# Six weight units of a decoder layer split in halves, one evacuation that signals apart, one update ahead of a subtraction

## The chip, the cores and the metric

The kernel runs on one core of one Trainium2 chip. The metric is the device time of one launch in microseconds (us); three launches of the kernel before gave a median of 1365.99 us (1365.53 to 1366.52).

## What is computed

One decoder layer in float32 on 256 tokens of width 2048. Three token mixers read one input projection; their outputs are gated, merged, projected and normalised, and a mixture of 16 experts follows:

```python
h = x @ w_in[l]
(q_a, k_c, v_c, k_s, v_s, k_w, v_w, g_nsa, q_b, c_kv, q_idx, k_idx, w_idx,
 uv, g_merge) = _split_cols(h, IN_SPLITS)
...
y = jnp.einsum('bsnw,nwd->bsnd', branches, w_branch[l])
gates = jax.nn.sigmoid(g_merge.astype(jnp.float32)).astype(x.dtype).reshape(B, S, N_BRANCHES, D)
mixed = jnp.sum(gates * y, axis=2) @ w_out[l]
x = _layer_norm(DEEPNORM_ALPHA * x + mixed, ln1_g[l], ln1_b[l])
ffn = _hier_moe(x, router_group_w[l], router_group_b[l], router_expert_w[l], router_expert_b[l],
                expert_w_gate[l], expert_w_up[l], expert_w_down[l])
x = _layer_norm(DEEPNORM_ALPHA * x + ffn, ln2_g[l], ln2_b[l])
```

Inside the first mixer, blocks of 32 keys and of 32 values are each compressed by a product of 4096 values with `cmp_w1` (`jax.nn.gelu(xb @ w1) @ w2`).

## The kernel before

**Units.** Up to the experts, every weight is read in units of 128 x 2048 float32 (1 MB). A unit passes four stations. SyncE (SP) loads it into one of six slots of `raw`. ScalarE (ACT) copies it to `whi` as fp32r, the high part (`hi`, L1470). VectorE (DVE) subtracts, `wlo = raw - whi`, the low part (`lo`, L1699). TensorE (PE) multiplies: each product is three matmuls, high by high, high by low and low by high (`mm3`, L1065 to L1067). `whi` and `wlo` have two slots each, so the copy of unit u waits until PE has used unit u - 2.

**Signals.** `landed` counts loads, `hi_done` copies, `lo_done` subtractions, `unit_used` units that PE has finished. PE waits for `lo_done` before a unit (`unit_ready`). Unit 0 alone is already worked in quarters, with the semaphores `part_hi` and `part_lo` (`first_part`, L1574 and L1824), and PE waits for a quarter in the middle of that unit.

**Order.** Each engine runs a program written out by hand. First come 13 chunks of the input projection (NCH = 13), of four units each but for one: ckv (units 0 to 3), small (4), kcvc (5 to 8), slc (9 to 12), then four units of `cmp_w1` (13 to 16, `w1u` = 13), win (17 to 20), and qa0 to u1. A unit of a chunk is 48 matmuls of 256 columns or 24 of 512, a unit of `cmp_w1` only 12 of 512 columns. Chunks alternate between two accumulators, `main[0]` and `main[1]`. When PE has finished a chunk, ACT moves it out (`evacuate`) and increments `chunk_out`. The last chunk, u1, is moved out by two gelus (L1509) from `main[0]`; then the loop of steps begins.

**Steps.** For each of three branches b and four blocks i of 512 columns, `step(b, i)` multiplies four units of gate columns into `main[1]` and two units of `w_branch` into `main[0]`. At its start PE waits for `chunk_out` >= NCH + 4b + i. After its first unit PE computes attention scores (L1272), which need `qst`, two copies that ACT makes at the head of its own step (L1629). In the fifth position DVE adds sigmoid times product to the merged sum `acc` (L1932, L1933), after the low part of the unit two ahead, and increments `step_free`. Branches 0 and 1 run in hardware loops, and so do three steps of the last branch; its last step is written out (there `i` is a Python integer).

**Output projection and experts.** Unit U1 is the first of `w_out`. After it PE transposes the last columns of the merged sum (`merged(3)`, L1338), which waits for `step_free`. The experts (`moe_pe`) stream 192 units of 1 MB through a ring of places; SP loads a unit when PE has used the one that lay there (`m_used`).

Two lines that decide the first waits of a step, on PE and on DVE:

```python
pe.wait_ge(chunk_out, NCH + it + i)
dve.wait_ge(chunk_out, NCH + 1 + 4 * b + i)
```

Of the kernel before, what the change touches and what calls it, by code (L numbers as in the profile page):

```python
# [17 lines left out]
F32, F32R, I32 = mybir.dt.float32, mybir.dt.float32r, mybir.dt.int32  # L18
# [40 lines left out]
UNIT = 2048  # L59
# [28 lines left out]
def build(nc, A, out):  # L88
# [14 lines left out]
    with ExitStack() as ctx:  # L103
        def sem(name):
            return ctx.enter_context(nc.semaphore(name))
# [38 lines left out]
        UB = QUADS + 2  # L144
        BR = [2, 0, 1]
        U1 = U0 + NB * 4 * UB
        assert UB % RAW == 0 and UB % SPLIT == 0

        def last(name):
# [144 lines left out]

        landed = [sem(f"landed{j}") for j in range(RAW)]
        hi_done, lo_done, unit_used = sems("hi_done lo_done unit_used")
        chunk_out = sem("chunk_out")
        step_free = sem("step_free")

        pch, ach, dch = sems("pch ach dch")  # L300
# [742 lines left out]
        def _(pe):  # L1043
# [34 lines left out]
            def unit_ready(u):  # L1078
                pe.wait_ge(lo_done, u + 1)

            def start_chunk(name):
                c = chunks[name][0]
                if c >= 2:
                    pe.wait_ge(chunk_out, c - 1)
                return main[c % 2], chunks[name][1]
# [17 lines left out]
            def mixed_chunk(name, f0, t0, hook=None):  # L1103

                ps, u0 = start_chunk(name)
                for q in range(QUADS):
                    u = u0 + q
                    if u:
                        unit_ready(u)
                    if u and name == "ckv":  # L1110
                        pe.wait_ge(x_lo, 2 * q + 2)
                    wh, wl = view(whi, u % SPLIT, 4, 512), view(wlo, u % SPLIT, 4, 512)
                    for kk in range(4):
                        k = 4 * q + kk
                        if u == 0:
                            if kk % 2 == 0:
                                pe.wait_ge(x_lo, kk // 2 + 1)
                            if kk < 3:
                                pe.wait_ge(part_lo, kk + 1)
                            else:  # L1120
                                unit_ready(0)
                        for m in range(2):
                            c = f0 + m * P
                            features(ps[:, 0, m * S:(m + 1) * S], k, wh[:, kk, c:c + P], wl[:, kk, c:c + P],
                                     k == 0 and m == 0, k == KT - 1, True)
                        for t in range(T):
                            ins = tokens(ps[:, 1, t * 256:(t + 1) * 256], k, t, wh[:, kk, t0:t0 + 256],
                                         wl[:, kk, t0:t0 + 256], k == 0 and t == 0, k == KT - 1, True)
                        if u == 0 and kk == 1:
                            x_transposes(range(2, 4))  # L1130
                    ins.then_inc(unit_used, 1)
                    if hook:
                        hook(u)
# [67 lines left out]
            for j, (xh, xl) in enumerate(((xpkh, xpkl), (xpvh, xpvl))):  # L1201
                pe.wait_ge(xp_lo, j + 1)
                for q in range(2):
                    u = w1u + 2 * j + q
                    unit_ready(u)
                    wh, wl = view(whi, u % SPLIT, 16, P), view(wlo, u % SPLIT, 16, P)
                    for l in range(0, 16, LB):
                        cols = slice((q * 16 + l) * KV * NC, (q * 16 + l + LB) * KV * NC)
                        ins = mm3(att[0:LB * KV * NC, 3 - 2 * j, :], xh[:, cols], xl[:, cols],
                                  wh[:, l:l + LB, :].rearrange("p l m -> p (l m)"),  # L1210
                                  wl[:, l:l + LB, :].rearrange("p l m -> p (l m)"), q == 0 and l == 0,
                                  q == 1 and l == 16 - LB)
                    ins.then_inc(unit_used, 1)
# [128 lines left out]
            def step(b, i):  # L1342
                ub, it = U0 + b * 4 * UB, 4 * b
                src = (o1, o2, o1)[b]
                g, y = NCH % 2, (NCH + 1) % 2
                for j in range(UB):
                    u = ub + j
                    if j == 0:
                        pe.wait_ge(chunk_out, NCH + it + i)
                    if j == QUADS:  # L1350
                        pe.wait_ge(step_free, 1 + it + i)
                        if b == 2:
                            pe.wait_ge(att_free, 9)
                    pe.wait_ge(lo_done, u + 1 + i * UB)
                    wh, wl = view(whi, u % SPLIT, 4, 512), view(wlo, u % SPLIT, 4, 512)
                    for kk in range(4):
                        for t in range(T):
                            if j < QUADS:
                                k = 4 * j + kk
                                ins = tokens(main[g][:, t, :], k, t, wh[:, kk, :], wl[:, kk, :], k == 0, k == KT - 1)  # L1360
                            else:
                                k = 4 * (j - QUADS) + kk
                                cols = slice(t * P, (t + 1) * P)
                                ins = mm3(main[y][:, t, :], src[:, 0, k, cols], src[:, 1, k, cols],
                                          wh[:, kk, :], wl[:, kk, :], k == 0, k == HEADS - 1)
                    ins.then_inc(unit_used, 1)
                    if b == 0:
                        if j == 0:
                            pe.wait_ge(att_free, 1 + i)
                            scores(1 + i, True)  # L1370
                        if j == 3:
                            transposes(1 + i, True)
                        if j == 4:
                            values(1 + i, True)
                    if b == 1:
                        if j == 0:
                            pe.wait_ge(att_free, 5 + i)
                            latent_kv(i, 1 + i)
                        if j == 1:
                            pe.wait_ge(kh_out, 1 + i)  # L1380
                            pe.wait_ge(vh_out, 1 + i)
                            scores(5 + i, False)
                        if j == 3:
                            transposes(5 + i, False)
                        if j == 4:
                            values(5 + i, False)
                    if b == 2 and isinstance(i, int) and j < 3:
                        merged(j)
# [26 lines left out]
                    ins.then_inc(lt_ps, 1)  # L1415


            pe.wait_ge(chunk_out, NCH + 12)
            for c in range(4):
                ps = main[(NCH + c) % 2]  # L1420
                if c >= 2:
# [40 lines left out]
        def _(act):  # L1462
# [9 lines left out]
            def hi_at(u):  # L1472
                if u == SMALL:
                    act.wait_ge(gn_in, 16)
                hi(u, u % RAW, n=(KT * NSM if u == SMALL else UNIT), wait=u - SPLIT + 1 if u >= SPLIT else None)

            def evacuate(name):
# [28 lines left out]
                else:  # L1506
                    for j in range(2):
                        g = int(name[1]) * 4 + j * 2
                        ins = act.activation(flat(uT[:, g:g + 2, :]), ps[:, j, :], ACT.Gelu_apprx_tanh)  # L1509
                    ins.then_inc(chunk_out, 1)  # L1510

            after = {}
            for name in chunks:
# [180 lines left out]
        def _(dve):  # L1694
# [5 lines left out]
                                  ALU.subtract).then_inc(lo_done, 1)  # L1700

            def lo_at(u):
                lo(u, u % RAW, u + 1, KT * NSM if u == SMALL else UNIT)

            def qseg(tensor, q):
# [132 lines left out]
                    x_part(2 * u + 3)  # L1838
                extra(u)
            lo_at(U0)  # L1840
            dve.wait_ge(chunk_out, NCH)
            dve.tensor_tensor(mixt[:, 4:8, :], mixt[:, 4:8, :], uT[:, 4:8, :], ALU.mult).then_inc(mix_u, 1)
            lo_at(U0 + 1)
            dve.wait_ge(oc_hi, 1)
# [54 lines left out]
                                      mhi[dst].rearrange("p k s -> p (k s)").bitcast(F32), ALU.subtract).then_inc(m_lo, 1)  # L1899

            def step(b, i):
                for j in range(UB):
                    u = U0 + b * 4 * UB + j + 2
                    lo(u, u % RAW, u + 1 + i * UB)
                    if b == 0:
                        if j == 0:
# [10 lines left out]
                    if b < 2 and j == 4:  # L1917
# [3 lines left out]
                            ins = dve.tensor_tensor(dst[:, 1, bass.ds(4 * a + i, 1), :].rearrange("p a s -> p (a s)"), att[:, a, 0:S],  # L1921
                                                    dst[:, 0, bass.ds(4 * a + i, 1), :].rearrange("p a s -> p (a s)").bitcast(F32), ALU.subtract)
                        ins.then_inc(att_free, 1)
                    if j == 5:
                        dve.wait_ge(chunk_out, NCH + 1 + 4 * b + i)
                        dve.wait_ge(unit_used, u - 1 + i * UB)
                        a_ = acc[:, :, bass.ds(i * 512, 512)]
                        y = main[(NCH + 1) % 2]
                        if b == 0:
                            dve.tensor_tensor(a_, sig[:], y[:], ALU.mult).then_inc(step_free, 1)  # L1930
                        else:
                            link(dve.tensor_tensor(sig[:], sig[:], y[:], ALU.mult))  # L1932
                            dve.tensor_tensor(a_, a_, sig[:], ALU.add).then_inc(step_free, 1)  # L1933
                    if b == 2 and isinstance(i, int) and 1 <= j < 4:
                        merged(j - 1)

# [30 lines left out]
```

## Time and profile before

| | us |
|---|---|
| median of 3 runs | 1365.99 |
| the profiled execution, its own time | 1364.78 |
| its span | 1362.8 |
| PE busy | 1321.0 (97%) |
| weight loads of PE busy, 7311 of them (beside the matmuls) | 967.0 (71%) |
| DVE busy | 581.8 (43%) |
| ACT busy | 482.2 (35%) |
| granted PE clock, mean | 0.995 |

The span is the time between the first and the last instruction that the profiler saw; the launch's own time is 2.0 us more. Busy time counts instructions that run; a wait is idle time, and the profile names the instruction that ended it. A row of the timeline gives start, duration, engine, line and tiles, and in brackets the idle time before it with its releaser. Ends of matmuls are modelled, so the spacing of their starts says more than their durations.

### The profile page before, as it was taken

What the parts mean: (1) busy time and instruction counts of PE and PEld (TensorE: products, weight loads), DVE (VectorE), ACT (ScalarE), POOL (GpSimd) and SP (SyncE); (2) the same over time, 40 slices, a digit from 0 to 9 for tenths busy, and PEclk for the clock granted to TensorE, in tenths of its full rate; (3) what the DMA queues carried; (4) which work ended last, traced back from release to release, by engine and by line L of the source; (5) the groups of instructions that cost most, each with busy time, mean ns of one, the idle gap of its engine ahead of it and who ended that gap; (6) DMA issues with size and microseconds to landing.
All of it is one profiled execution on the core that took longest, in us unless ns stands there. A gap on an engine that the chain in (4) does not pass through costs nothing.

```text
span 1362.8 us, 17747 instructions
## 1 busy us (share of the span) xinstructions
PE 1321.0 (97%) x7311; PEld 967.0 (71%) x7311; DVE 581.8 (43%) x738; ACT 482.2 (35%) x658; POOL 27.5 (2%) x45
## 2 busy tenths in 40 slices
PE   8999999999999999999999999999999999999895
PEld 8989989998888888888888878854443443544341
DVE  4377445445546535545454554525121120211206
ACT  4544334335455544545333433331111111211111
POOL 0000000400000000000100001000000000000000
PEclk9999999999999999999999999999999999999998
DMA  9767555544444356545556795699999999999995
GB/s 302 257 191 240 185 185 186 186 156 157 156 150 154 124 169 189 166 168 169 183 187 194 274 381 202 241 372 388 412 421 421 422 421 421 422 419 422 421 404 194
DMA packets 120460, 364.94 MB, mean 268 GB/s; under 512 B 11528, under 2 KB 17096, under 8 KB 96336
## 3 DMA queue, kind: packets, MB, share of 16 engines
q1 hardware_dynamic: 114080, 359.58, 71.1%
q10 hardware_dynamic: 6320, 4.49, 1.1%
q8 instruction: 46, 0.75, 0.2%
q14 instruction: 14, 0.11, 0.0%
HBM read 361.95 MB, written 2.10 MB: 267 GB/s over the span
## 4 chain that ended last, share of the span: by engine, by line
PE 90%; DMA 5%; DVE 2%; ACT 1%; issue 1%; DVEq 0%; SPq 0%; ACTq 0%
PE main L1065 19%; PE main L1067 18%; PE main L1066 18%; PE main L501 14%; PE att L567 6%; DMA mraw<-in_expert_w_down_dram 5%; PE att L458 4%; PE att L1304 1%; PE att L1272 1%; PE main L470 1%; PE main L471 1%; PE att L550 1%; PE att L1287 1%; ACT whi L1470 1%; PE att L1323 1%
## 5 line engine op out<-in xcount | busy, mean ns | idle before, releaser
L1699 DVE TENSOR_TENSOR wlo<-raw,whi 128x2048 fp32r<-128x2048 f32 (+1 forms) x140 | 321.9, 2299 | 371.4 <-ACT whi L1470 371.4
L1470 ACT ACTIVATE whi<-raw 128x2048 fp32r<-128x2048 f32 (+1 forms) x140 | 267.6, 1911 | 430.9 <-PE main L1067 423.9
L501 PE MATMUL main<-mraw,xg 128*64 128x512 f32 x1024 | 225.0, 594 | 0.1
L1065 PE MATMUL main<-whi,xhi 128*128 128x512 f32 (+1 forms) x544 | 203.5, 374 | 1.3 <-ACT uT L1509 1.3
L1067 PE MATMUL main<-whi,xlo 128*128 128x512 f32 (+1 forms) x544 | 201.7, 371 | 0.0
L1066 PE MATMUL main<-wlo,xhi 128*128 128x512 f32 (+1 forms) x544 | 201.5, 370 | 0.0
L501 PEld LDWEIGHTS main<-mraw,xg 128*64 128x64 f32 x1024 | 71.9, 137 | 135.9 <-issue 134.6
L1065 PE MATMUL main<-xhi,whi 128*128 128x256 f32 (+1 forms) x560 | 159.6, 285 | 2.2 <-DVE wlo L1699 1.1
L1066 PE MATMUL main<-xlo,whi 128*128 128x256 f32 (+1 forms) x560 | 158.4, 283 | 0.0
L1067 PE MATMUL main<-xhi,wlo 128*128 128x256 f32 (+1 forms) x560 | 158.4, 283 | 0.0
L1065 PEld LDWEIGHTS main<-whi,xhi 128*128 128x128 f32 x544 | 102.6, 189 | 18.4 <-issue 1.5
L1067 PEld LDWEIGHTS main<-whi,xlo 128*128 128x128 f32 x544 | 102.5, 188 | 17.8
L1066 PEld LDWEIGHTS main<-wlo,xhi 128*128 128x128 f32 x544 | 102.6, 189 | 17.0
L1065 PEld LDWEIGHTS main<-xhi,whi 128*128 128x128 f32 (+1 forms) x560 | 106.9, 191 | 4.0 <-DVE wlo L1699 1.5
L1066 PEld LDWEIGHTS main<-xlo,whi 128*128 128x128 f32 (+1 forms) x560 | 106.9, 191 | 0.0
L1067 PEld LDWEIGHTS main<-xhi,wlo 128*128 128x128 f32 (+1 forms) x560 | 106.9, 191 | 0.0
L567 PE MATMUL att<-mraw,hT 128*64 128x512 f32 x448 | 98.6, 594 | 3.9 <-DMA mraw<-in_expert_w_down_dram 3.4
L608 ACT ACTIVATE xg<-att,gbT 128x128 f32<-128x128 f32 x128 | 47.3, 465 | 133.0 <-PE att L458 132.7
L567 PEld LDWEIGHTS att<-mraw,hT 128*64 128x64 f32 x448 | 31.9, 137 | 66.2 <-issue 62.8
L755 DVE TENSOR_TENSOR out_acc<-out_acc,main 128x512 f32<-128x512 f32 x64 | 41.4, 684 | 83.4 <-PE main L471 67.1
L1065 PE MATMUL main<-whi,o 128*128 128x512 f32 x192 | 76.4, 398 | 0.0
L1067 PE MATMUL main<-whi,o 128*128 128x512 f32 x192 | 74.9, 390 | 0.0
(319 smaller groups left out, 1352.7 us busy)
## 6 DMA issues: line engine op xcount, KB each, us to landing
raw<-in_w_in_dram SPq DMA_DIRECT2D x95, 1024.0 KB, 5.0
mraw<-in_expert_w_gate_dram SPq DMA_DIRECT2D x64, 1024.0 KB, 19.2
mraw<-in_expert_w_up_dram SPq DMA_DIRECT2D x64, 1024.0 KB, 20.8
mraw<-in_expert_w_down_dram SPq DMA_DIRECT2D x64, 1024.0 KB, 17.7
raw<-in_w_branch_dram SPq DMA_DIRECT2D x24, 1024.0 KB, 5.1
raw<-in_w_out_dram SPq DMA_DIRECT2D x16, 1024.0 KB, 7.0
xin<-in_x_dram SPq DMA_DIRECT2D x4, 512.0 KB, 8.1
out_dram<-out_acc SPq DMA_DIRECT2D x8, 256.0 KB, 2.0
```

The costliest lines, as they stand in the source:

```text
L458: ins = pe.matmul(att[:, q, k % 4 * P:(k % 4 + 1) * P], xr[:, t, k * P:(k + 1) * P], hot[:, t, :], start=(k % 4 == 0 and t == 0), stop=(t ...
L470: pe.matmul(main[1][:, n % 2, :], rows, yhi[:, c % 2, :], start=True, stop=False)
L471: pe.matmul(main[1][:, n % 2, :], rows, ylo[:, c % 2, :], start=False, stop=True).then_inc(sc_ps, 1)
L501: ins = pe.matmul(main[0][half, w, :], xg[:, k, half], src[:, kk * DE:(kk + 1) * DE], start=(k == 0), stop=(k == KT - 1))
L567: ins = pe.matmul(att[half, c, :], hT[:, f, half], src[:, c * 512:(c + 1) * 512], start=(f == 0), stop=(f == DE // P - 1))
L608: ins = act.activation(xg[:, k, :], att[:, q, k % 4 * P:(k % 4 + 1) * P], ACT.Identity, bias=gbT[:, KT + k:KT + k + 1], scale=gbT[:, k:k + 1])
L755: dve.tensor_tensor(out_acc[:, t, cols], out_acc[:, t, cols], main[1][:, n % 2, :], ALU.add).then_inc(sc_free, 1)
L1065: pe.matmul(o, ah, bh, start=start, stop=False, skip_group_check=skip)
L1066: pe.matmul(o, ah, bl, start=False, stop=False, skip_group_check=skip)
L1067: return pe.matmul(o, al, bh, start=False, stop=stop, skip_group_check=skip)
L1470: act.activation(whi[:, u % SPLIT, 0:n], raw[:, slot, 0:n], ACT.Copy).then_inc(hi_done, 1)
L1699: dve.tensor_tensor(wlo[:, u % SPLIT, 0:n], raw[:, slot, 0:n], whi[:, u % SPLIT, 0:n].bitcast(F32), ALU.subtract).then_inc(lo_done, 1)
```

## The change

Three edits. Unit 1, the four units of `cmp_w1` and the first unit of win (`HALVED`, units 1 and 13 to 17) are copied, subtracted and waited for in two halves of 1024 columns; the first halves signal through `part_hi` and `part_lo`, whose counts go on from unit 0's. The evacuation of u1 increments a semaphore of its own, `u1_out`, and every later count of `chunk_out` is one less. In the step that is written out, DVE's update of the merged sum stands before the subtraction of the unit it followed.

```diff
+        HALVED = [1, *range(w1u, w1u + 5)]
...
+            def half_ready(u, half):
+
+                if half == 0 and u in HALVED:
+                    pe.wait_ge(part_lo, 4 + HALVED.index(u))
+                else:
+                    unit_ready(u)
...
-                        unit_ready(u)
+                        half_ready(u, 0)
...
+                        if kk == 2 and u in HALVED:
+                            half_ready(u, 1)
...
-                    unit_ready(u)
                     wh, wl = view(whi, u % SPLIT, 16, P), view(wlo, u % SPLIT, 16, P)
                     for l in range(0, 16, LB):
+                        if l % 8 == 0:
+                            half_ready(u, l // 8)
...
-                        pe.wait_ge(chunk_out, NCH + it + i)
+                        pe.wait_ge(chunk_out, NCH - 1 + it + i)
...
+                if u in HALVED:
+                    act.wait_ge(landed[u % RAW], 16 * (u // RAW + 1))
+                    if u >= SPLIT:
+                        act.wait_ge(unit_used, u - SPLIT + 1)
+                    for cols, done in ((slice(0, UNIT // 2), part_hi), (slice(UNIT // 2, UNIT), hi_done)):
+                        act.activation(whi[:, u % SPLIT, cols], raw[:, u % RAW, cols], ACT.Copy).then_inc(done, 1)
+                    return
...
-                    ins.then_inc(chunk_out, 1)
+                    ins.then_inc(u1_out if name == "u1" else chunk_out, 1)
...
-            dve.wait_ge(chunk_out, NCH)
+            dve.wait_ge(u1_out, 1)
...
                 for j in range(UB):
                     u = U0 + b * 4 * UB + j + 2
+                    if j == 5 and isinstance(i, int):
+                        update(u)
                     lo(u, u % RAW, u + 1 + i * UB)
...
+                    if j == 5 and not isinstance(i, int):
+                        update(u)
```

`lo_at` has a loop like that of `hi_at`, with two subtractions. `update` holds DVE's two products as they stood.

**ACT, behind unit 14.** The queue from the end of slc's evacuation (`vs`) to the copy of unit 18; `cT` is a transposed latent. Before:

```order
L1494 ACTIVATE vs<-main 128x512
L1470 ACTIVATE whi<-raw 128x2048 [waits unit_used,landed3]
L1538 ACTIVATE cT<-att 128x512 [waits c_ps]
L1470 ACTIVATE whi<-raw 128x2048 [waits unit_used,landed4]
L1470 ACTIVATE whi<-raw 128x2048 [waits unit_used,landed5]
L1470 ACTIVATE whi<-raw 128x2048 [waits unit_used,landed0]
```

Now:

```order
L1512 ACTIVATE vs<-main 128x512
L1491 ACTIVATE whi<-raw 128x1024 [waits unit_used,landed3]
L1491 ACTIVATE whi<-raw 128x1024
L1556 ACTIVATE cT<-att 128x512 [waits c_ps]
L1491 ACTIVATE whi<-raw 128x1024 [waits unit_used,landed4]
L1491 ACTIVATE whi<-raw 128x1024
L1491 ACTIVATE whi<-raw 128x1024 [waits unit_used,landed5]
L1491 ACTIVATE whi<-raw 128x1024
L1481 ACTIVATE whi<-raw 128x2048 [waits unit_used,landed0]
```

Each copy of the units 15, 16 and 17 has become two, with the waits on the first of the two; what stands between the units stands where it did.

**DVE, in the last step.** The queue around the update of the merged sum (`sig`, then `acc`); `mlo` is the low part of the merged sum, transposed. Before:

```order
L1699 TENSOR_TENSOR wlo<-raw,whi 128x2048 [waits hi_done] x2
L1932 TENSOR_TENSOR sig<-sig,main 128x1024 [waits unit_used,chunk_out]
L1933 TENSOR_TENSOR acc<-acc,sig 128x2x512 [waits dch]
L1699 TENSOR_TENSOR wlo<-raw,whi 128x2048 [waits hi_done]
L1898 TENSOR_TENSOR mlo<-att,mhi 128x512 [waits m_hi] x2
```

Now:

```order
L1717 TENSOR_TENSOR wlo<-raw,whi 128x2048 [waits hi_done]
L1936 TENSOR_TENSOR sig<-sig,main 128x1024 [waits unit_used,chunk_out]
L1937 TENSOR_TENSOR acc<-acc,sig 128x2x512 [waits dch]
L1717 TENSOR_TENSOR wlo<-raw,whi 128x2048 [waits hi_done] x2
L1923 TENSOR_TENSOR mlo<-att,mhi 128x512 [waits m_hi] x2
```

The subtraction of unit U1 + 1 has gone from ahead of the two products to behind them.

## Rows read from the trace of the kernel before

**Rows 1.** Waits of PE over the whole span: us in total, times, longest.

```profile
PE att L1065 <- DVE wlo L1699: 2.9, 2, 1.5
...
PE att L1338 <- DVE acc L1933: 1.3, 1, 1.3
PE main L1065 <- ACT uT L1509: 1.3, 1, 1.3
PE main L1065 <- DVE wlo L1699: 1.1, 1, 1.1
```

**Rows 2.** Windows: length; busy us of PE, PEld, DVE, ACT, POOL; clock, DMA share, GB/s.

```profile
895.00:900.00 5.00, 5.00 (x25) 1.44 (x21) 0.00 (x0) 0.00 (x0) 0.00 (x0) 1.00 0.43 144
...
950.00:960.00 10.00, 10.00 (x54) 4.82 (x52) 1.28 (x2) 1.50 (x4) 0.00 (x0) 1.00 0.87 341
...
1180.00:1190.00 10.00, 10.00 (x59) 5.07 (x58) 0.48 (x1) 1.50 (x4) 0.00 (x0) 1.00 1.01 422
```

**Rows 3.** Timeline around unit 1, PE, ACT and DVE, 8 to 24 us.

```profile
12.98 1.91 ACT L1470 ACTIVATE whi<-raw 128x2048 fp32r<-128x2048 f32 x1
...
14.93 2.29 DVE L1699 TENSOR_TENSOR wlo<-raw,whi 128x2048 fp32r<-128x2048 f32 x1 [1.00 <-ACT whi L1470]
...
17.27 0.39 PE L1065 MATMUL main<-xhi,whi 128*128 128x256 f32 x1 [1.11 <-DVE wlo L1699]
...
20.03 2.29 DVE L1699 TENSOR_TENSOR wlo<-raw,whi 128x2048 fp32r<-128x2048 f32 x1 [1.61 <-ACT whi L1470]
...
23.92 0.36 PE L1065 MATMUL main<-xhi,whi 128*128 128x256 f32 x1
```

**Rows 4.** Timeline over the units 14 to 17, PE, ACT and DVE, 91 to 106 us.

```profile
91.13 1.92 ACT L1470 ACTIVATE whi<-raw 128x2048 fp32r<-128x2048 f32 x1 [4.30 <-PE main L1067]
...
93.08 2.29 DVE L1699 TENSOR_TENSOR wlo<-raw,whi 128x2048 fp32r<-128x2048 f32 x1 [1.79 <-ACT whi L1470]
...
95.43 0.50 PE L1065 MATMUL att<-whi,xpkh 128*120 128x512 f32 x1 [1.50 <-DVE wlo L1699]
...
102.87 0.49 PE L1065 MATMUL att<-whi,xpvh 128*120 128x512 f32 x1 [1.39 <-DVE wlo L1699]
...
105.96 0.35 PE L1065 MATMUL main<-xhi,whi 128*128 128x256 f32 x1
```

**Rows 5.** Timeline: operations of 960 columns on ACT and DVE, at 81 to 91 us.

```profile
80.86 0.99 ACT L1535 ACTIVATE xpkh<-xpk 128x960 fp32r<-128x960 f32 x1
...
90.14 1.15 DVE L1773 TENSOR_TENSOR xpvl<-xpv,xpvh 128x960 fp32r<-128x960 f32 x1
```

**Rows 6.** Timeline of PE inside unit 0: the second row begins its second quarter.

```profile
9.81 0.28 PE L1067 MATMUL main<-whi,xlo 128*128 128x256 f32 x1
9.93 0.28 PE L1065 MATMUL main<-xhi,whi 128*128 128x256 f32 x1
```

**Rows 7.** Timeline where the steps begin, PE and ACT, 318 to 326 us.

```profile
318.29 1.09 ACT L1509 ACTIVATE uT<-main 128x512 f32<-128x512 f32 x2 [3.78 <-PE main L1067]
...
319.51 0.49 PE L1065 MATMUL main<-whi,xhi 128*128 128x512 f32 x1 [1.26 <-ACT uT L1509]
...
324.30 0.73 ACT L1629 ACTIVATE qst<-qaT 128x256 f32 x2
...
325.17 0.89 PE L1272 MATMUL att<-ksT,qst 128*128 128x128 f32 x4
```

**Rows 8.** Timeline around the last step's end, ACT, DVE and PE, 784 to 792 us.

```profile
784.31 1.92 ACT L1470 ACTIVATE whi<-raw 128x2048 fp32r<-128x2048 f32 x1 [3.52 <-PE main L1067]
...
786.26 2.29 DVE L1699 TENSOR_TENSOR wlo<-raw,whi 128x2048 fp32r<-128x2048 f32 x1 [3.15 <-ACT whi L1470]
788.47 1.21 DVE L1932 TENSOR_TENSOR sig<-sig,main 128x1024 f32<-128x1024 f32 x1
789.72 1.23 DVE L1933 TENSOR_TENSOR acc<-acc,sig 128x1024 f32<-128x1024 f32 x1
...
791.00 1.09 PE L1338 MATMUL att<-ident,acc 128*128 128x128 f32 x8 [1.34 <-DVE acc L1933]
```

More of the change, by code:

```diff
@@ L296, in build @@
         hi_done, lo_done, unit_used = sems("hi_done lo_done unit_used")
-        chunk_out = sem("chunk_out")
+        chunk_out, u1_out = sem("chunk_out"), sem("u1_out")
         step_free = sem("step_free")
@@ L1415, in route @@
                     ins.then_inc(lt_ps, 1)
-            pe.wait_ge(chunk_out, NCH + 12)
+            pe.wait_ge(chunk_out, NCH + 11)
             for c in range(4):
@@ L1702, in lo_at @@
             def lo_at(u):
+                if u in HALVED:
+                    for cols, made_, value, done in ((slice(0, UNIT // 2), part_hi, 4 + HALVED.index(u), part_lo),
+                                                     (slice(UNIT // 2, UNIT), hi_done, u + 1, lo_done)):
+                        dve.wait_ge(made_, value)
+                        dve.tensor_tensor(wlo[:, u % SPLIT, cols], raw[:, u % RAW, cols], whi[:, u % SPLIT, cols].bitcast(F32),
+                                          ALU.subtract).then_inc(done, 1)
+                    return
                 lo(u, u % RAW, u + 1, KT * NSM if u == SMALL else UNIT)
@@ L1901, in step, with update @@
             def step(b, i):
+                def update(u):
+                    dve.wait_ge(chunk_out, NCH + 4 * b + i)
+                    dve.wait_ge(unit_used, u - 1 + i * UB)
+                    a_ = acc[:, :, bass.ds(i * 512, 512)]
+                    y = main[(NCH + 1) % 2]
+                    if b == 0:
+                        dve.tensor_tensor(a_, sig[:], y[:], ALU.mult).then_inc(step_free, 1)
+                    else:
+                        link(dve.tensor_tensor(sig[:], sig[:], y[:], ALU.mult))
+                        dve.tensor_tensor(a_, a_, sig[:], ALU.add).then_inc(step_free, 1)
                 for j in range(UB):
                     u = U0 + b * 4 * UB + j + 2
+                    if j == 5 and isinstance(i, int):
+                        update(u)
                     lo(u, u % RAW, u + 1 + i * UB)
@@ L1923, in step @@
                         ins.then_inc(att_free, 1)
[L1924 to L1933, printed above, removed]
+                    if j == 5 and not isinstance(i, int):
+                        update(u)
                     if b == 2 and isinstance(i, int) and 1 <= j < 4:
```

## The prediction

> **What bounds the kernel now.** I read the waits of PE first. PE is busy 97% of the span, so only its idle time can go, and up to the experts its list holds few waits: 2.9 us in two waits of `cmp_w1` units for their low part, 1.1 in one wait of a unit of ckv for the same, 1.3 where the steps begin, for a gelu of u1, and 1.3 where the transposes of the merged sum wait for DVE's last product [rows 1]. That is 6.6 us in all, and the change touches every one of them. The first question is which of them really go.
>
> The second question is whether time won early arrives at the end, and for that I read the windows of the expert stage. There the DMA engines are the pace: at 1180 us they move 422 GB/s at a share of 1.01, while between 895 and 900 us they moved 144 GB/s and between 950 and 960 us 341 [rows 2]. So the stream has holes at its start, where SP waits for places that PE has yet to free, and runs without them later. A stream that starts to run full when PE lets it start moves with PE. All of its gates (units used of `w_out`, places used by the first experts) lie behind the four waits. I therefore carry every microsecond won before 800 us through to the end, one for one.
>
> **Unit 1.** The whole copy starts at 12.98 and takes 1.91, the subtraction starts at 14.93 and takes 2.29, and PE starts at 17.27 after 1.11 idle, so it was ready at 16.16 [rows 3]. For a half of 1024 columns I take the rows of 960 columns, 0.99 on ACT and 1.15 on DVE [rows 5], and between these and the rows of 2048 columns about 1.04 and 1.22. The first half is then low at 12.98 + 1.04 + 1.22 + 0.05 for the handoff = 15.3, before 16.16. The second half follows some 1.2 behind it, at 16.5, and PE wants it half a unit after its start, at 19: unit 2 starts 6.65 after unit 1, with eight transposes between, so a unit of 48 matmuls takes about 5.8. The wait goes whole: 1.1. What is late next is unit 2, whose subtraction ends at 20.03 + 2.29 = 22.32 because its copy came late; PE started it at 23.92 and will want it at 22.8 [rows 3]. There is 0.5 us left, so nothing is given back.
>
> **Units 13 to 17.** The copy of unit 14 starts at 91.13, when PE has released the slot, the subtraction at 93.08, and PE starts at 95.43, 1.50 late, so it was ready at 93.93 [rows 4]. With halves the first is low at 91.13 + 1.04 + 1.22 + 0.05 = 93.4 and the second at about 94.6. PE reaches the second half six matmuls later, at half of the 3.09 that a unit takes from its start to the next unit's (102.87 to 105.96, [rows 4]), thus at 95.5. Both are in time, by 0.5 and 0.9. From here on a slot is released a unit earlier relative to the old chain. The copy of unit u starts when unit u - 2 ends, its first half is low 2.3 later, and PE wants it 3.09 later: a margin of 0.7 per unit, where the whole chain of 1.92 + 2.29 = 4.2 missed by 1.1. That covers units 15 and 16, and also unit 17, which before had the time that the wait of unit 16 gave it and would now be the next late one if it were whole. Unit 18 is whole, but PE works unit 17, a long one, for 5.8, more than 4.2. So both waits go: 1.50 + 1.39 = 2.9. I take off 0.1 for the break that PE keeps at a unit's start and book 2.8.
>
> The splits add one instruction per unit on ACT and on DVE, twelve in all. Between 960 and 2048 columns ACT's time grows by 0.93 us and DVE's by 1.14 for 1088 columns [rows 3, 5], so a column costs 0.85 and 1.05 ns and the part that does not grow is 0.17 and 0.14 us. That is at most 0.3 us per unit, and it lies beside PE: with 2.1 us of ACT and 2.4 of DVE in the 3.09 of a unit both queues have room.
>
> PE gets six more waits in the middle of a unit. Unit 0 has such waits already: its second quarter begins 0.12 after the matmul before, the spacing inside a quarter [rows 6]. I book nothing; the upper bound is one weight load uncovered at each, 0.13 us by the page (967.0 us in 7311 loads), 0.8 in all. The Trainium skill, "TensorE: Matmul & The Clock Gate", section on queue depths, says that PE's queue can pull weight loads ahead of matmuls in flight. If a wait closed that window, each of the six would cost up to such a load, and the sum would be 4.4; rows 6 speak against it.
>
> **The signal of u1.** Step 0 writes `main[1]`, whose chunk u0 was moved out long before, so PE no longer waits for the gelus and starts at 318.25 in place of 319.51. That looks like 1.26 us. But the step's first unit is followed by the scores, and these need `qst`. ACT's way there is one chain that starts at u1's end and that the edit leaves alone: two gelus from 318.29, a copy, the high part of the mixed output, a table load, and the two `qst` copies, 324.30 + 0.73 = 325.03. PE's scores ran at 325.17 [rows 7]. Before, PE and ACT met there by chance. Now PE is there 1.26 earlier, at 323.9, and waits 1.2 us for ACT. What is late next is `qst`, and I book 0 us, within bounds of 0 and 1.3. I take the lower end because ACT's chain has no gap that PE's start could close.
>
> **The merged sum.** PE's unit U1 - 1 ends at 784.3, where ACT's copy of unit U1 + 1 is released [rows 8]. DVE idles then. Before, it waited for that copy, subtracted from 786.26, and only then ran the products, 788.47 and 789.72 to 790.95; PE had waited 1.34 when it started at 791.00, so it was ready at 789.66. Now the products run at 784.35 to 786.85 and the subtraction from 786.9 to 789.15. PE finds the sum 2.8 us before it wants it, and its next unit's low part 1.6 us before it wants that (789.66 + 1.09 = 790.75). The gain is 1.3. The subtraction ends 0.6 later, and SP's next load of `w_out`, which waits for it, starts 0.6 later, for a unit that is due five units on.
>
> **Sum.** 1.1 + 2.8 + 0 + 1.3 = 5.2 us. The profiled execution, 1364.78, would be 1359.6. It is 1.2 below the median, and a difference carries over: 1365.99 - 5.2 = **1360.8**.
>
> **The rivals.** *The first signal pays in full.* If `qst` were not the gate, because PE's own time to the scores is longer than I read or ACT starts earlier, the 1.3 of rows 7 would come on top: 1359.5. The 0.14 us between `qst` and the scores is all that speaks for it.
>
> *The halves move their waits.* My margins in units 14 to 17 are 0.5 to 0.9 us per unit. The Trainium skill, "VectorE: DVE Perf Modes", section on the trn2 errata, says that many small tiles each pay a fixed latency that one large tile pays once; rows 5 agree with some 0.15 us. If copies and subtractions do not overlap as I laid them out and each half arrives 0.7 late, the waits shrink to about a half and unit 17 gets one: 1.4 of 2.8 is lost, and 1362.2 comes out.
>
> *The expert stream does not follow.* If its start is set by something that does not move with PE (its own queue at 800 us, say), the end stays where it is, 1366. The holes of rows 2 speak against it.
>
> *Slower.* The stream's holes grow. The one between 950 and 960 us costs 10 x (1 - 341/422) = 1.9 us [rows 2]. PE now meets the ring of places at another phase of SP's waits, and a place freed late in each expert pair would open one more such hole per pair. Against a gain of 5.2 it takes (5.2 + 2.7) / 1.9, thus more than four new holes, to come out slower; with five, 1365.99 - 5.2 + 9.5 = 1370.3. Nothing in the trace shows a hole once PE is well ahead.
>
> **How the numbers follow.** About 0.2% (2.7 us, thus 1363.3) is what a measurement can tell from no change. Forecast 0.68; first signal in full 0.09; waits moved 0.11; stream does not follow 0.09; slower 0.03. The first three are faster: 0.88; the fourth is the same, 0.09. The range holds the first three with the bounds of the mid-unit waits and half a microsecond of scatter: 1359.0 to 1363.0.
>
> **What would show it.** PE's list of waits should have lost the waits for `wlo` at units 1, 14 and 16 and the one for `acc`. The wait for uT should be gone too, and a new one of about 1.2 us stand before the scores, for `qst` on ACT: this is the sharpest sign. The unit that follows the `cmp_w1` units should start 3.9 us earlier than before, at 102.1. The stream should again show 422 GB/s at 1180 us and end 5 us earlier. A wait on `part_lo` in units 14 to 17, or breaks of 0.2 us in their middle, would show the halves mis-sized. No new wait before the scores, with a span 6.5 us shorter, would show my reading of `qst` wrong; an unchanged end of the stream would break the step that carries gains through.

## The result, and the profile after

The changed kernel took 1358.36 us (median of 4, 1357.47 to 1358.89) against 1366.13 for the kernel before (median of 4); the ratio is 0.9947 with a 95% interval of 0.9935 to 0.996, so 5.5 to 8.9 us faster. The forecast of 1360.8 named the places of the gain rightly, but the time lies 0.6 us below the low end of its range. The profiled execution took 1358.89, the longest of the four, with a span of 1357.2 against 1362.8.

The list of PE's waits, over the whole span, answers to [rows 1]. Of the four groups there, none is left; one wait is new:

```profile
PE main L538 <- DVE hh L764: 8.6, 8, 1.1
...
PE att L1283 <- ACT qst L1647: 1.5, 1, 1.5
PE main L1066 <- DVE wlo L1849: 1.0, 1, 1.0
```

The wait for `wlo` L1849 is unit 0's and stood in the trace before too. The new one, for `qst`, is where the forecast put it, and it takes the whole gain of the first signal.

Timeline of the changed kernel around unit 1, against [rows 3] (start, duration, engine, line, tiles):

```profile
13.21 2.01 ACT L1491 ACTIVATE whi<-raw 128x1024 fp32r<-128x1024 f32 x2
...
14.31 2.36 DVE L1725 TENSOR_TENSOR wlo<-raw,whi 128x1024 fp32r<-128x1024 f32 x2
...
15.35 1.04 PE L1056 MATMUL att<-ident,xin 128*128 128x128 f32 x8
16.14 0.36 PE L1066 MATMUL main<-xhi,whi 128*128 128x256 f32 x1
...
18.13 1.92 ACT L1481 ACTIVATE whi<-raw 128x2048 fp32r<-128x2048 f32 x1 [1.06 <-DMA raw<-in_w_in_dram]
```

Two halves of a copy take 2.01 in place of 1.91, two of a subtraction 2.36 in place of 2.29: the split costs 0.1 and 0.07 us, less than the bound of 0.3 for both. PE goes from the transposes into unit 1 without idle time.

The same over the `cmp_w1` units, the first matmul of each of the units 13 to 17, against [rows 4]:

```profile
89.74 0.47 PE L1066 MATMUL att<-whi,xpkh 128*120 128x512 f32 x1
...
92.61 0.39 PE L1066 MATMUL att<-whi,xpkh 128*120 128x512 f32 x1
...
95.41 0.46 PE L1066 MATMUL att<-whi,xpvh 128*120 128x512 f32 x1
...
98.28 0.39 PE L1066 MATMUL att<-whi,xpvh 128*120 128x512 f32 x1
...
101.06 0.30 PE L1066 MATMUL main<-xhi,whi 128*128 128x256 f32 x1
```

A unit now takes 2.8 to 2.9 us from start to start, about twelve times 0.233, the usual spacing of these matmuls. The five starts span 11.32 us; before, from 90.90 to 105.96 [rows 4], they spanned 15.06. That is 3.74 us, where the sum booked 2.8. Unit 17, which the forecast expected at 102.1 us, starts at 101.06. Two places of the kernel before, in its own timeline, show what the list of waits had left out:

```profile
93.55 0.39 PE L1067 MATMUL att<-whi,xpkl 128*120 128x512 f32 x1
95.43 0.50 PE L1065 MATMUL att<-whi,xpkh 128*120 128x512 f32 x1 [1.50 <-DVE wlo L1699]
95.77 0.39 PE L1066 MATMUL att<-wlo,xpkh 128*120 128x512 f32 x1
...
96.04 2.29 DVE L1699 TENSOR_TENSOR wlo<-raw,whi 128x2048 fp32r<-128x2048 f32 x1 [0.67 <-ACT whi L1470]
...
98.08 0.40 PE L1067 MATMUL att<-whi,xpkl 128*120 128x512 f32 x1
98.48 0.46 PE L1065 MATMUL att<-whi,xpvh 128*120 128x512 f32 x1
```

The idle time of 1.50 is counted from the modelled end of a matmul, 93.55 + 0.39. But the next start was due 0.23 after the last, at 93.78, so 1.65 us were lost. The matmul behind it starts 0.34 us later, where 0.23 is usual. At 98.48 no wait is listed, and the start is 0.17 late all the same: PE was due at 98.31, and DVE had unit 15's low part ready at 96.04 + 2.29 = 98.33.

Where the steps begin, against [rows 7]:

```profile
313.34 1.09 ACT L1527 ACTIVATE uT<-main 128x512 f32<-128x512 f32 x2 [3.78 <-PE main L1068]
...
316.12 1.92 ACT L1619 ACTIVATE o<-mixt 128x2048 fp32r<-128x2048 f32 x1
318.06 1.28 ACT L1647 ACT_TABLE_LOAD   x1
319.35 0.73 ACT L1647 ACTIVATE qst<-qaT 128x256 f32 x2
...
320.22 0.89 PE L1283 MATMUL att<-ksT,qst 128*128 128x128 f32 x4 [1.45 <-ACT qst L1647]
```

ACT's chain from u1's end to `qst` is as long as before (6.74 us from 313.34 to 320.08; before, 318.29 to 325.03), and PE starts the scores 0.14 behind it, as before.

At the last step's end, against [rows 8]:

```profile
779.51 1.22 DVE L1936 TENSOR_TENSOR sig<-sig,main 128x1024 f32<-128x1024 f32 x1 [1.21 <-PE main L1068]
780.77 1.23 DVE L1937 TENSOR_TENSOR acc<-acc,sig 128x1024 f32<-128x1024 f32 x1
781.91 2.28 DVE L1717 TENSOR_TENSOR wlo<-raw,whi 128x2048 fp32r<-128x2048 f32 x1
...
784.69 1.04 PE L1349 MATMUL att<-ident,acc 128*128 128x128 f32 x8
```

The transposes no longer wait. The expert stream again runs at 423 GB/s at 1180 us, against 422 in [rows 2]:

```profile
1180.00:1190.00 10.00, 10.00 (x58) 4.88 (x56) 2.05 (x9) 1.84 (x6) 0.00 (x0) 1.00 1.02 423
```

### The profile page after: what moved, and what is told of

The parts are those of the page before. It is cut to its first block, busy times and chain, and to the rows that moved or that the text cites. A ratio compares the mean times of both kernels' runs of the same rounds, so it can differ in the third digit from the quotient of the medians.

```text
span 1357.2 us, 17759 instructions
## 1 busy us (share of the span) xinstructions
PE 1321.8 (97%) x7311; PEld 969.0 (71%) x7311; DVE 582.3 (43%) x744; ACT 483.3 (36%) x664; POOL 27.5 (2%) x45
## 4 chain that ended last, share of the span: by engine, by line
PE 92%; DMA 5%; DVE 1%; ACT 1%; issue 1%; DVEq 0%; SPq 0%; ACTq 0%
PE main L1066 19%; PE main L1068 19%; PE main L1067 19%; PE main L502 14%; PE att L568 6%; DMA mraw<-in_expert_w_down_dram 5%; PE att L459 4%; PE att L1315 1%; PE att L1283 1%; PE main L471 1%; PE main L472 1%; PE att L551 1%; PE att L1298 1%; PE att L1334 1%; PE att L1330 1%
## 5 line engine op out<-in xcount | busy, mean ns | idle before, releaser
L1717 DVE TENSOR_TENSOR wlo<-raw,whi 128x2048 fp32r<-128x2048 f32 x134 | 308.1, 2299 | 359.5 <-ACT whi L1481 359.5
L1481 ACT ACTIVATE whi<-raw 128x2048 fp32r<-128x2048 f32 x134 | 256.3, 1913 | 418.1 <-PE main L1068 416.3
L756 DVE TENSOR_TENSOR out_acc<-out_acc,main 128x512 f32<-128x512 f32 x64 | 41.4, 684 | 83.7 <-PE main L472 67.2
```

The source lines that it names most:

```text
L756: dve.tensor_tensor(out_acc[:, t, cols], out_acc[:, t, cols], main[1][:, n % 2, :], ALU.add).then_inc(sc_free, 1)
L1481: act.activation(whi[:, u % SPLIT, 0:n], raw[:, slot, 0:n], ACT.Copy).then_inc(hi_done, 1)
L1717: dve.tensor_tensor(wlo[:, u % SPLIT, 0:n], raw[:, slot, 0:n], whi[:, u % SPLIT, 0:n].bitcast(F32), ALU.subtract).then_inc(lo_done, 1)
```

## The experiments

Each kernel was timed against the kernel before on the same chip. The first theory (the forecast's) takes listed waits, 1.1, 2.8, 0 and 1.3; the second, formed on the trace after, takes starts. From the start of unit 0 the traces give, in us, the start of: unit 13, unit 17, the scores, the transposes of the merged sum, and the router's first matmul (the fold, L425 or L426):

| trace | unit 13 | unit 17 | scores | transposes | fold |
|---|---|---|---|---|---|
| before | 82.47 | 97.53 | 316.74 | 782.57 | 871.30 |
| changed | 81.08 | 92.40 | 311.56 | 776.03 | 864.71 |
| halves only | 81.12 | 92.40 | 311.55 | 777.39 | 866.14 |
| signal only | 82.48 | 97.57 | 316.80 | 782.62 | 871.37 |
| update only | 82.48 | 97.53 | 316.74 | 781.07 | 869.75 |

So up to the fold the three edits give 5.16, -0.07 and 1.55 us, 6.64 together, and the changed kernel 6.59 (6.7 and 6.8 when it was traced again). Up to there traces of one kernel agree within 0.2: the kernel before, traced again, gave 82.47, 97.56, 316.78, 782.73 and 871.47.

**The changed kernel again, twice** (no edit).

> The changed kernel as it stands, timed again beside the others. If its profile tells the whole gain, its median lies some 5.6 us (the difference of the two profiled spans) below the kernel before; if the executions that were not profiled hold some 2 us more than the waits show, it lies 7 to 8 us below.

> The changed kernel a third time, beside the next one on the same chip. By the start-to-start theory (1.2 + 3.7 + 0 + 1.4) it stands 6.3 us below the kernel before; its first two measurements gave 7.2 and 7.9. If the rest is scatter of the expert stage, this one may fall on either side of 6.3 to 8; if it is a gain of its own, it stays above 7.

Measured: 1357.89 us against 1365.81, ratio 0.9942 (0.9929 to 0.9956), then 1357.76 against 1365.32, ratio 0.9942 (0.9928 to 0.9956). With the first measurement the ratios give 7.2, 7.9 and 7.9 us. The listed-wait sum of 5.2 is outside all three intervals (the nearest bound is 5.5). The 6.6 of the starts is inside all three, but each value lies above it.

**Only the halves.**

```diff
-                    ins.then_inc(u1_out if name == "u1" else chunk_out, 1)
+                    ins.then_inc(chunk_out, 1)
...
-                    if j == 5 and isinstance(i, int):
-                        update(u)
...
-                    if j == 5 and not isinstance(i, int):
+                    if j == 5:
                         update(u)
```

(and each count of `chunk_out` one higher again).

> Only the six units in halves; the signal of u1 and the order of the last step as before. The start-to-start readings of the changed trace give 1.2 us at unit 1 and 3.7 us at the units 13 to 16, so 4.9 us faster. My prediction's terms give 3.9. If the halves hold the part that was missed, 6 or more.

Measured: 1359.43 us, ratio 0.9959 (0.9946 to 0.9973), thus 5.6 us (3.7 to 7.4). The interval alone does not part 4.9 from 3.9 or from 6; the trace does, with 5.16 at the fold. That is over three quarters of the 6.6 of the whole change.

**Only the signal.**

```diff
-        HALVED = [1, *range(w1u, w1u + 5)]
+        HALVED = []
```

and the order of the last step as before.

> Only the signal of u1 apart. By the theory that qst takes the place of the gelu as the gate: 0 us, with a new wait of 1.2 to 1.5 us before the scores. By the rival that the signal pays: 1.3 us faster and no such wait.

Measured: 1364.99 us, ratio 0.9997 (0.9988 to 1.0006), 0.4 us within -0.8 and 1.6. The interval still holds the rival's 1.3, so the trace has to decide. It has the swap with nothing else moving: the wait for the gelu is gone from PE's list, and this stands there:

```profile
PE att L1283 <- ACT qst L1647: 1.4, 1, 1.4
```

The scores start 316.80 us after unit 0, where they started at 316.74 before. The signal by itself brings nothing.

**Only the update, twice.** `HALVED = []` and the counts of `chunk_out` as before.

> Only the update of the merged sum ahead of the subtraction in the last step. By the theory: 1.3 us faster. If the expert stream takes some of it, or the last step holds the missed 2 us, less than 1 or more than 2.5.

> Only the update moved, again: by the theory 1.4 us faster; if the 2.2 us of its first measurement are a gain of its own in the expert stage, 2 or more again.

Measured: 1363.3 us, ratio 0.9984 (0.9975 to 0.9993), then 1363.28, ratio 0.9986 (0.9977 to 0.9995), thus 2.2 and 1.9 us. The traces show 1.55 and 1.56 at the fold. Both times agree with that; neither excludes 0.5 us more.

**The units 13 to 17, and 13 to 16.**

```diff
-        HALVED = [1, *range(w1u, w1u + 5)]
+        HALVED = [*range(w1u, w1u + 5)]
```

and for the second kernel `w1u + 4`, both with the signal and the update as before.

> Only the units 13 to 17 in halves, nothing else. Start-to-start theory: 3.7 us faster. My prediction's term: 2.8.

> Only the units 13 to 16 in halves, unit 17 whole. By the theory that unit 17 becomes the next late one: its copy starts when unit 15 ends, some 100 us, and it is low 4.3 later, while PE wants it after 2.8, so a new wait of about 1.4 us stands before win, and 2.3 us are gained of the 3.7. By the rival that unit 17 did not need it: 3.7.

Measured: 1361.57 us, ratio 0.9971 (0.9959 to 0.9983), 4.0 us (2.3 to 5.6); and 1363.63, ratio 0.9988 (0.9979 to 0.9997), 1.6 us (0.4 to 2.9). The first interval does not part 3.7 from 2.8; the second excludes 3.7. In the first trace unit 17 starts 93.82 after unit 0, in the second 95.62, and in the kernel before 97.53: gains of 3.71 and 1.91. Unit 17 is in the list for a reason. In the second trace it is the next late unit (DVE's subtractions of the units 17 and 18, PE's last matmul of unit 16 and its start of unit 17):

```profile
101.48 2.29 DVE L1717 TENSOR_TENSOR wlo<-raw,whi 128x2048 fp32r<-128x2048 f32 x1 [1.34 <-ACT whi L1481]
104.27 2.29 DVE L1717 TENSOR_TENSOR wlo<-raw,whi 128x2048 fp32r<-128x2048 f32 x1 [0.49 <-ACT whi L1481]
...
101.83 0.40 PE L1068 MATMUL att<-whi,xpvl 128*120 128x512 f32 x1
103.92 0.36 PE L1066 MATMUL main<-xhi,whi 128*128 128x256 f32 x1 [1.69 <-DVE wlo L1717]
```

The wait that was moved is listed with 1.69, where I had put 1.4, and start to start it is 1.86 (103.92 less 101.83 and 0.23). I had let unit 17's copy start together with unit 16; it began at 99.54, 0.27 us after unit 16's first matmul. Unit 18, whole in both, starts on time.

**A delay ahead of the steps.** This kernel computes all that the kernel before does and adds idle matmuls.

```diff
+            pe.wait_ge(att_free, 1)
+            keep_warm(pe, 184)
             for b in range(NB):
                 with pe.Fori(0, 4 if b < 2 else 3) as i:
```

> The kernel before with 184 idle matmuls of 128 columns (some 0.115 us each, 21.2 us) on PE ahead of the first step. If time is carried one for one through the expert stream: they take the wait of 1.3 us for the gelu with them, and the time grows by 19.9 us. If the stream swallows part of what comes before it: less. If a microsecond ahead of the stream is worth more than one at the end (the missed part of the gain being in proportion, 7.3 for 6.3): 23.

The delay was twice what I had written, since a matmul of this kind is two in the trace:

```profile
318.70 41.26 PE L417 MATMUL att<-ident 128*128 128x128 f32 x368
...
359.71 0.48 PE L1065 MATMUL main<-whi,xhi 128*128 128x512 f32 x1
```

The step starts at 359.71 in place of 319.51, so 40.2 later. But unit 0 started 0.6 later in this execution too (9.04 in place of 8.43); counted from unit 0, the step is 39.6 later, the scores and the fold 39.5. Measured: 1404.77 against 1364.68, ratio 1.0289 (1.0274 to 1.0303), 39.4 us (37.4 to 41.4). So the time goes through to the end one for one, within 2 us. A stream that swallows more than that does not fit, nor one that multiplies by 7.3 / 6.3 (46 us).

**The mixed output's high part on DVE, twice.** The changed kernel, with ACT's chain to `qst` cut:

```diff
-            act.wait_ge(mix_u, 2)
-            act.activation(o1[:, 0].rearrange("p h s -> p (h s)"), mixt[:].rearrange("p g s -> p (g s)"),
-                           ACT.Copy).then_inc(oc_hi, 1)
...
+            dve.wait_ge(mix_u, 2)
+            dve.tensor_copy(o1[:, 0].rearrange("p h s -> p (h s)"), mixt[:].rearrange("p g s -> p (g s)")).then_inc(oc_hi, 1)
```

> The changed kernel, with the high part of the mixed output made by DVE instead of ACT, so that ACT reaches qst about 1.9 us sooner. By the theory that qst is the gate that took the signal's gain: the wait of 1.45 us before the scores goes, and the time falls by 1.3 to 1.5 against the changed kernel, thus to about 8.7 below the kernel before. By the rival that this wait is worth nothing at the end (the expert stream being the bound): as the changed kernel.

> The copy on DVE again, now against the changed kernel on the same chip: 1.4 to 1.8 us below it (its trace showed the scores 1.8 us earlier relative to the start), or no difference if the wait for qst is not worth its length.

In the first trace `qst` is done at 318.04, 0.3 us before PE takes it up, and the scores follow the last product without a gap:

```profile
317.31 0.73 ACT L1644 ACTIVATE qst<-qaT 128x256 f32 x2
...
318.15 0.40 PE L1068 MATMUL main<-whi,xlo 128*128 128x512 f32 x1
318.38 0.82 PE L1283 MATMUL att<-ksT,qst 128*128 128x128 f32 x4
```

The scores start 310.07 after unit 0, 1.5 less than in the changed kernel: `qst` was the gate. (The 1.8 of the second expectation was counted from the span's start; unit 0 was 0.35 earlier in this execution.) The fold comes at 863.05, 1.7 sooner. The times are less clear. The first gave 1357.81 against 1364.68, ratio 0.9943 (0.9929 to 0.9956); the second, beside the changed kernel on one chip, 1357.21 against its 1357.76, ratios 0.994 and 0.9942. So at most half a microsecond shows in the medians, and the intervals, 3.7 us wide, can't part that from 1.5. Among executions of the same mean granted clock more shows: on the chip of the second pair, at 0.995, three of this kernel average 1356.5 us and four of the changed kernel 1357.8. These are few. The second trace gives one reason for its part. PE's start of unit 2, and the copy it waits on:

```profile
23.59 0.38 PE L1066 MATMUL main<-xhi,whi 128*128 128x256 f32 x1 [0.91 <-DVE wlo L1714]
...
19.30 1.91 ACT L1481 ACTIVATE whi<-raw 128x2048 fp32r<-128x2048 f32 x1 [2.56 <-DMA raw<-in_w_in_dram]
```

Unit 2's copy began at 19.30, not 18.13, as its load landed later in this execution, and unit 2 waited 0.91 us. The forecast had left unit 2 a margin of 0.5. Unit 13 starts 82.25 after unit 0 here, so of unit 1's gain of 1.4 us only 0.2 was left. This happened in one of the six traces that have unit 1 in halves; how often it happens in other executions stays open.

**The kernel before against itself.**

> The kernel before against itself, as a control: no difference, 0 within the interval. Its trace gives a second reading of the expert stage from the first gather to the last down product (434.3 us in the first trace): if this stage alone scatters by 1 to 2 us from execution to execution, the 0.9 us that the changed kernel gained beyond its start-to-start shift need no cause of their own.

Measured: 1365.64 against 1365.73, ratio 1.0 (0.9991 to 1.0009). From the router's fold on, executions differ though. The gather of the first expert starts 9.5 us after the fold in most traces and 10.1 in four of them, and from there to the last pair's last down products the two traces of the kernel before take 434.3 and 434.5 us, the three of the changed kernel 434.2, 436.3 and 433.8, and all traces without the delay lie between 432.7 and 436.8. The last section shows what most of this goes with.

## Why the prediction fell short

**What bounds the kernel, and carrying gains through:** right. The delay, 39.5 us at the fold, came out as 39.4 within 2. The rival in which the stream does not follow is out, and so is the slower one: the kernel is faster in all three measurements.

**Unit 1, booked 1.1:** right in mechanism, small in size. The traces give 1.4 to unit 13 (82.47 less 81.08). PE's listed 1.11 is counted from the modelled end of the transposes; in the changed trace unit 1 starts 0.79 after them, so before, at 15.92 in place of 17.27, 1.35 was lost. The margin of unit 2 held in all traces with unit 1 in halves but one.

**Units 13 to 17, booked 2.8: the term that failed.** It measured 3.74. I summed two idle times, and took 0.1 off for a break at a unit's start. Start to start the two waits were 1.65 and 1.56 us, not 1.50 and 1.39, and the units 15 and 17 started 0.2 late each with no wait listed. These four make 3.6; the rest lies mostly in the matmul behind each of the two listed waits, which started 0.1 us later than is usual. The Trainium skill ("Perfetto Trace Analysis", on TensorE) says that the profiler estimates the end of a matmul and does not observe it; the trace agrees: matmuls that start every 0.233 us are listed with 0.39 or 0.40, so each ends after the next has begun. The break that I took to belong to PE was a wait for DVE too: unit 15 started 0.15 us after DVE had its low part, and in the changed trace twelve matmuls take 2.8 us and the next unit follows at once. The rows for it stood in my own account, which had 3.09 us from unit 16's start to unit 17's, when twelve times the spacing is 2.8. That the halves come in time, and that unit 17 is late if whole, held. The margins did not, as they rested on the same 3.09. DVE's two halves of unit 15 in the changed trace:

```profile
94.04 2.36 DVE L1725 TENSOR_TENSOR wlo<-raw,whi 128x1024 fp32r<-128x1024 f32 x2 [0.94 <-ACT whi L1491]
```

The first half takes 1.23 of the 2.36 and is low at 95.27, and PE starts the unit at 95.41. By the same reading the units 14, 16 and 17 have 0.6, 0.3 and 0.2 us. The forecast had 0.5 at unit 14 and 0.7 at each of the others.

**The splits and the mid-unit waits, booked at nothing:** right. A unit takes its twelve times the spacing with the wait in its middle, and the splits cost 0.17 us per unit beside PE. The result of 4.4 that I had worked out by the Trainium skill ("TensorE: Matmul & The Clock Gate", queue depths) did not come: no weight load was uncovered.

**The first signal, booked 0:** right, by the wait for `qst` of 1.45 us and by the trace of the kernel with the signal alone. The rival that it pays in full is out. Had I booked its 1.3 us, the forecast would have been 1359.5, nearer the measured time for a wrong reason.

**The merged sum, booked 1.3:** the transposes start 1.36 us sooner between the scores and them (465.83 less 464.47), and 1.5 to 1.7 from unit 0 with this edit alone. Nothing was late behind it.

**The sum.** With starts in place of listed waits it is 1.4 + 3.7 + 0 + 1.4 = 6.5, thus 1359.5. That is inside the range, but 1.1 above the first measurement. Half of this was my base: 1365.99 is 0.6 above the mean of all the timings of the kernel before, some eighty (1365.4), which gives 1358.9. The medians of the change (1358.36, 1357.89, 1357.76) lie 0.5 to 1.1 below that.

The clock that PE was granted goes with most of this rest. Among executions whose mean granted clock was 0.995, 24 of the kernel before average 1364.6 us and 9 of the changed kernel 1357.9. At 0.994, 38 and 2 average 1365.7 and 1358.9. Both differences are 6.8, what the traces show at the fold (6.6 to 6.8). For the update alone, the comparison at 0.995 gives 1.5, and its starts 1.55. Of the kernel before, 52 of 78 executions were at 0.994 or 0.993, of the changed kernel 3 of 14. Whether the change makes the lower clock rarer, or chance did, no run here shows.

So of the 2.4 us between 1360.8 and 1358.36, 1.3 are terms too small (0.9 at the units 13 to 17, 0.3 at unit 1, 0.1 at the merged sum), 0.6 the base, and the rest goes with the clock. The range was too narrow at its low end: it allowed half a microsecond of scatter, where the interval of a measured ratio is 1.7 to 1.9 us to either side.

## What to carry to other kernels

Cost a wait by starts: the late start less the last start and the usual spacing. The idle time before a matmul is counted from a modelled end and left out 0.15 to 0.25 us at each of three waits here, and two short ones of 0.2 altogether. A little more, 0.1 us at each of two waits, stood behind the late start; the span over several starts, before and after, has it all.

When a wait goes, follow the engine that ended it to the next thing it owes. The signal on its own was free of the gelu and met the same queue one unit later, and the halves had to be carried one unit further than the listed waits, to unit 17.

Splitting a copy and a subtraction in two cost 0.17 us of two engines that had room, and made 4.2 us of latency 2.3. It paid in the units of 2.8 us, which are shorter than the chain of 4.2, and at unit 1, for which PE was ready at 15.92 and the chain only at 17.27.

## What the runs showed of the hardware

In some executions PE's granted clock fell to its lower level, 1.2 GHz, in the router's stage and in others of the same kernel not. Windows of the idle matmuls there, in the changed kernel and in the kernel before traced again (length; busy us of PE, PEld, DVE, ACT, POOL; clock, DMA share, GB/s):

```profile
877.00:880.00 3.00, 3.00 (x15) 3.00 (x15) 2.31 (x14) 3.00 (x2) 0.00 (x0) 0.50 1.02 421
```

```profile
884.00:887.00 3.00, 3.00 (x16) 3.00 (x16) 2.49 (x14) 3.00 (x2) 0.00 (x0) 0.54 0.98 407
```

The first trace of the kernel before had 1.00 there:

```profile
883.00:886.00 3.00, 3.00 (x29) 3.00 (x29) 2.53 (x14) 2.99 (x2) 0.00 (x0) 1.00 1.03 431
```

What PE did before it was the same in all three: small products of 20 columns and transposes, with 0.33 us of idle time. The price is 0.6 us: the gather starts 10.1 us after the fold in the four traces with such a fall, and 9.5 in the ten others.

In two of these ten the clock fell later, during the gather. One is the changed kernel timed again; here beside its third measurement, over the same stretch:

```profile
882.00:886.00 4.00, 3.62 (x19) 3.66 (x20) 3.52 (x24) 1.70 (x3) 0.00 (x0) 0.61 1.01 428
```

```profile
882.00:886.00 4.00, 3.59 (x33) 3.43 (x32) 3.54 (x23) 2.98 (x9) 0.00 (x0) 1.00 1.01 426
```

From the fold to the end of the span these two traces take 485.1 and 486.2 us, the four with the fall before the gather 483.8 to 484.4, and the eight with neither 482.2 to 483.1. So most of the scatter of 4 us between executions goes with whether, and where, the clock fell in this stage.
